# A transformer block on one core: four gate units as seven half-size products (Strassen) in place of eight

## What is computed

```python
proj = xn @ w_in                       # 1024 x 4808
qa, ka, va, qi, ki, wi, qb, kb, vb, ga, gb = split(proj)
oa = dsa_attention(...)                # sparse attention, keys chosen by the scores of qi, ki
ob = stick_breaking_attention(qb, kb, vb)
merged = sigmoid(ga) * (oa @ w_proj_a) + sigmoid(gb) * (ob @ w_proj_b)
h = x + merged @ w_out
h = h + moe_ffn(rms_norm(h))           # 32 experts, 12.58 MB of weights each
```

## Time and profile before

| | |
|---|---|
| median of 3 runs | 1138.24 us (1136.64 to 1138.38) |
| the profiled execution | 1135.92 us, span 1134.1 us |
| TensorE busy | 1090.9 us, 96% of the span |
| VectorE, ScalarE, GpSimd busy | 262.5, 139.7, 8.4 us |
| TensorE clock granted, mean | 0.989 |
| HBM read | 434.89 MB, 384 GB/s over the span |

### The profile page before, as it was taken

One profiled execution on the slowest core, in us unless ns is written; L12 is line 12 of the kernel. 1 busy time (PEld: TensorE's weight loads), 2 busy tenths in 40 slices (PEclk: granted clock), 3 DMA queues, 4 the chain that ended last, 5 costly groups with the idle time before them and its releaser, 6 DMA issues.

```text
span 1134.1 us, 11423 instructions
## 1 busy us (share of the span) xinstructions
PE 1090.9 (96%) x5083; PEld 478.5 (42%) x5083; DVE 262.5 (23%) x619; ACT 139.7 (12%) x237; POOL 8.4 (1%) x16
## 2 busy tenths in 40 slices
PE   8999999999999999999999979999999999999997
PEld 5677778443333333333333324333333333333332
DVE  2665323242111111111111111221111111111111
ACT  1415332010000000000000000000000000000001
POOL 0100000000000000000000000000000000000000
PEclk9999999999999999999999998999999999999999
DMA  8365447799999999999999999999999999999996
GB/s 312 156 275 204 189 145 300 296 357 433 431 431 439 431 428 437 435 426 435 428 435 431 428 418 429 427 433 434 431 433 431 432 436 427 431 425 428 428 424 255
DMA packets 21506, 436.69 MB, mean 385 GB/s; under 512 B 2480, under 2 KB 2864, under 8 KB 6384
## 3 DMA queue, kind: packets, MB, share of 16 engines
q1 hardware_dynamic: 20496, 434.22, 90.4%
q10 hardware_dynamic: 960, 1.72, 0.4%
HBM read 434.89 MB, written 1.05 MB: 384 GB/s over the span
## 4 chain that ended last, share of the span: by engine, by line
PE 70%; DMA 24%; DVE 2%; SPq 2%; ACT 1%; issue 0%; ACTq 0%; DVEq 0%
PE Pp L927 31%; DMA gate_up_room<-in_w_gate_up 19%; PE Bp L941 11%; PE Pp L635 7%; PE Ap L955 3%; DMA odd_down<-in_w_down 3%; PE Pp L623 3%; PE Pp L809 2%; PE Ap L820 2%; PE Bp L913 2%; SPq L436 2%; DMA odd_down<-in_b_down 1%; PE Bp L934 1%; DVE odd_down L1457 1%; PE Pp L662 1%; PE Pp L869 1%
## 5 line engine op out<-in xcount | busy, mean ns | idle before, releaser
L927 PE MATMUL Pp<-gate_up_room,OBT 128*64 128x512 f32 x2048 | 453.3, 601 | 17.4 <-DMA gate_up_room<-in_w_gate_up 17.3
L927 PEld LDWEIGHTS Pp<-gate_up_room,OBT 128*64 128x64 f32 x2048 | 147.5, 139 | 307.1 <-issue 279.0
L1446 DVE TENSOR_SCALAR odd_down<-Pp 128x512 f32<-128x512 f32 x31 | 21.4, 692 | 622.2 <-PE Pp L927 622.2
L941 PE MATMUL Bp<-even_down,odd_down 128*64 128x512 f32 x512 | 113.7, 596 | 1.2
L941 PE MATMUL Bp<-odd_down 128*64 128x512 f32 x480 | 106.3, 595 | 1.8 <-DVE odd_down L1457 0.6
L635 PE MATMUL Pp<-odd_down,gate_up_room 128*128 128x256 f32 x384 | 85.2, 381 | 0.0
L1654 ACT ACTIVATE odd_down<-odd_down 128x512 f32<-128x512 f32 x30 | 18.9, 630 | 473.4 <-DVE odd_down L1446 473.4
L635 PEld LDWEIGHTS Pp<-odd_down,gate_up_room 128*128 128x128 f32 x384 | 72.2, 190 | 10.7 <-issue 1.1
L955 PE MATMUL Ap<-odd_down,cst 64*128 64x512 f32 x256 | 64.7, 624 | 4.9 <-DMA odd_down<-in_b_down 4.2
L941 PEld LDWEIGHTS Bp<-even_down,odd_down 128*64 128x64 f32 x512 | 35.2, 137 | 69.0 <-issue 63.3
L941 PEld LDWEIGHTS Bp<-odd_down 128*64 128x64 f32 x480 | 33.2, 137 | 65.3 <-issue 59.9
(11 more groups left out here) (209 smaller groups left out, 624.4 us busy)
## 6 DMA issues: line engine op xcount, KB each, us to landing
gate_up_room<-in_w_gate_up SPq DMA_DIRECT2D x27, 2048.0 KB, 42.5
even_down<-in_w_down SPq DMA_DIRECT2D x11, 4096.0 KB, 37.0
odd_down<-in_w_down SPq DMA_DIRECT2D x11, 4096.0 KB, 40.2
gate_up_room<-in_w_gate_up SPq DMA_DIRECT2D x10, 4096.0 KB, 22.0
gate_up_room<-in_w_in SPq DMA_DIRECT2D x8, 2048.0 KB, 7.4
even_down<-in_w_down SPq DMA_DIRECT2D x7, 2048.0 KB, 16.7
odd_down<-in_w_down SPq DMA_DIRECT2D x6, 2048.0 KB, 20.3
odd_down<-in_w_down SPq DMA_DIRECT2D x7, 1024.0 KB, 21.0
```

The source lines that it names most:

```text
L927: last = mm((Gps, Ups)[q // 2][64 * (q % 2):64 * (q % 2) + 64, :], xT[:, k % 4, k // 4, :], quarter(e, w, q), start=False, stop=k == KC - ...
L941: last = mm(bank[64 * hf:64 * hf + 64, :], turned[:, c, s, :], w[:, c * 1024 + hf * 512:][:, 0:512], start=s == 0 and c == 0, stop=s == DN ...
```

## The change

The product (2 x 2 blocks: feature block f of 256, contraction half k of 512, token block b of 128) is done for each pair of feature chunks, 128 features of each f, by seven products of 128 features x 512 x 128 tokens in place of eight, after Strassen (Winograd's form). GpSimd forms four differences of tokens once (`XS`, in the room of the bias rows) and four sums of weights per unit (`weight_sum`, in ring slots 0, 1 or 2, 3 by turns). ScalarE copies two partial results aside (`keep_products`), VectorE copies one (`gate_sum_6`), adds (`gate_sum_7`) and writes both chunks (`gate_last`). For each unit `gate_start` and `gate_end` stand where `column_half(u, 0)` and `column_half(u, 1)` stood. The unit's weights have three places now, the loads of units 6 to 9 come earlier, those of w_proj_b and w_out later. The diff, cut; where VectorE's and ScalarE's new calls stand is in its last parts:

```diff
+XS = norm_pair[:, 0:2048].rearrange("p (s k t) -> p s k t", s=4, k=4)
+kept = [cst[:, C_ADM:C_ADM + 384], once[:, 1624:2008]]
...
-    flat = slot(2, 0, 4096) if u == 2 else unit[:, u % 2, :]
+    flat = {2: slot(2, 0, 4096), 6: slot(4, 0, 4096), 7: unit[:, 0, :], 8: unit[:, 1, :],
+            9: slot(4, 0, 4096)}.get(u, unit[:, u % 2, :])
...
-    flat = unit[:, 0, :] if u == 10 else slot(4, 0, 4096)
+    flat = unit[:, u - 10, :]
...
+def weight_quarter(u, f, k):
+    return uview(u)[:, 4 * k:4 * k + 4, 256 * f:256 * f + 256]
+def weight_sum(u, i):
+    return slot(u % 2 * 2, 1024 * (i - 1), 1024).rearrange("p (k n) -> p k n", k=4)
+def token_quarter(k, b):
+    return XT[:, 4 * k:4 * k + 4, b * P:(b + 1) * P]
+def gate_chunk(t, f):
+    u = 6 + t // 2
+    return G[:, 4 * (u % 2) + t % 2 + 2 * f, (u - 6) // 2, :]
...
-    for u in range(11):
+    for u in (0, 1, 2, 3, 4, 6, 5, 7, 8, 9, 10, 11, 12):
         if u >= 3:
-            sp.wait_ge(m_half, 4 if u == 3 else 2 if u == 4 else 2 * (u - 1))
+            sp.wait_ge(m_half, {3: 4, 4: 2, 5: 8, 6: 2, 7: 10, 8: 12, 9: 14, 10: 16, 11: 18, 12: 18}[u])
...
-        if u >= 5 and u < 8:
-            load_unit(u + 6)
...
     for i in (1, 2, 3):
         load(0, i)
     load_half(0, 5, 1)
-    sp.wait_ge(bias_ok, 2)
+    sp.wait_ge(m_half, 20)
+    load_unit(13)
     load_half(1, 5, 0)
-    sp.wait_ge(m_half, 20)
+    load(0, 0)
+    sp.wait_ge(m_mg, KC)
     load(1, 1)
-    sp.wait_ge(m_mg, KC)
-    load(0, 0)
     load_half(0, 5, 0)
     load(1, 0)
...
+    def difference(dst, a, b, op, done):
+        nc.gpsimd.tensor_tensor(dst, a, b, op).then_inc(done, 1)
+    pool.wait_ge(v_sx, KC)
+    pool.wait_ge(bias_ok, 2)
+    difference(XS[:, 0], token_quarter(0, 1), token_quarter(0, 0), ALU.subtract, g_xs)
+    difference(XS[:, 2], token_quarter(1, 1), token_quarter(0, 1), ALU.subtract, g_xs)
+    pool.wait_ge(g_xs, 2)
+    difference(XS[:, 1], token_quarter(1, 1), XS[:, 0], ALU.subtract, g_xs)
+    pool.wait_ge(g_xs, 3)
+    difference(XS[:, 3], token_quarter(1, 0), XS[:, 1], ALU.subtract, g_xs)
+    for u in range(6, 10):
+        pool.wait_ge(unit_in[u], 16)
+        if u > 6:
+            pool.wait_ge(m_half, 6 if u == 7 else 2 * (u - 1))
+        n = 4 * (u - 6)
+        difference(weight_sum(u, 1), weight_quarter(u, 1, 0), weight_quarter(u, 1, 1), ALU.add, g_ws)
+        pool.wait_ge(g_ws, n + 1)
+        difference(weight_sum(u, 2), weight_sum(u, 1), weight_quarter(u, 0, 0), ALU.subtract, g_ws)
+        pool.wait_ge(g_ws, n + 2)
+        difference(weight_sum(u, 4), weight_quarter(u, 0, 1), weight_sum(u, 2), ALU.subtract, g_ws)
+        difference(weight_sum(u, 3), weight_quarter(u, 0, 0), weight_quarter(u, 1, 0), ALU.subtract, g_ws)
...
+    def product(t, part, w, x, start, stop):
+        f = slice(t % 2 * P, t % 2 * P + P)
+        for k in range(4):
+            last = mm(Pp[:, t % 2, part * P:(part + 1) * P], w[:, k, f], x[:, k, :], start=start and k == 0,
+                      stop=stop and k == 3, skip_group_check=True)
+        return last
...
+    def gate_products_15(t, u):
+        if t % 2 == 0:
+            pe.wait_ge(unit_in[u], 16)
+        product(t, 2, weight_quarter(u, 0, 0), token_quarter(0, 0), True, False)
+        if t == 0:
+            pe.wait_ge(g_xs, 4)
+        if t % 2 == 0:
+            pe.wait_ge(g_ws, 4 * (u - 6) + 1)
+        product(t, 1, weight_sum(u, 1), XS[:, 0], False, False).then_inc(m_p15, 1)
+    def gate_products_63(t, u):
+        pe.wait_ge(a_p15, t + 1)
+        if t % 2 == 0:
+            pe.wait_ge(g_ws, 4 * (u - 6) + 3)
+        product(t, 2, weight_sum(u, 2), XS[:, 1], False, False)
+        product(t, 1, weight_sum(u, 4), token_quarter(1, 1), False, True).then_inc(m_p63, 1)
+    def gate_product_7(t, u):
+        pe.wait_ge(v_p6, t + 1)
+        if t % 2 == 0:
+            pe.wait_ge(g_ws, 4 * (u - 6) + 4)
+        product(t, 2, weight_sum(u, 3), XS[:, 2], False, False).then_inc(m_p7, 1)
+    def gate_products_42(t, u):
+        pe.wait_ge(v_p7, t + 1)
+        product(t, 2, weight_quarter(u, 1, 1), XS[:, 3], False, True)
+        product(t, 0, weight_quarter(u, 0, 1), token_quarter(1, 0), False, True).then_inc(m_half, 1)
...
+    def gate_start(u):
+        a, b = 2 * u - 12, 2 * u - 11
+        if u == 6:
+            pe.wait_ge(a_half, 11)
+        else:
+            pe.wait_ge(v_gate, a - 1)
+        gate_products_15(a, u)
+        if u == 6:
+            pe.wait_ge(a_half, 12)
+        else:
+            pe.wait_ge(v_gate, a)
+        gate_products_15(b, u)
+        gate_products_63(a, u)
+    def gate_end(u):
+        a, b = 2 * u - 12, 2 * u - 11
+        gate_products_63(b, u)
+        gate_product_7(a, u)
+        gate_product_7(b, u)
+        gate_products_42(a, u)
+        gate_products_42(b, u)
...
-    column_half(6, 0)
+    gate_start(6)
     pe.wait_ge(a_half, 12)
     b_values(0)
     b_logits(1)
-    column_half(6, 1)
+    gate_end(6)
     b_sums(1)
-    column_half(7, 0)
+    gate_start(7)
     b_values(1)
     b_logits(2)
     turn_probabilities(1, 1)
-    column_half(7, 1)
+    gate_end(7)
     b_sums(2)
     a_values(1, 0, 1)
     head_products(QAT, KAT, 0, 2, P).then_inc(m_lg, 1)
-    column_half(8, 0)
+    gate_start(8)
     b_values(2)
     b_logits(3)
-    column_half(8, 1)
+    gate_end(8)
     b_sums(3)
     turn_probabilities(0, 2)
-    column_half(9, 0)
+    gate_start(9)
     b_values(3)
     a_values(0, 2, 2)
-    column_half(9, 1)
+    gate_end(9)
 
...
-            pe.wait_ge(a_half, nhalf[0] - 1 + c)
+            pe.wait_ge(v_gate, 7 + c)
...
+    def gate_sum_6(t):
+        dve.wait_ge(m_p63, t + 1)
+        V.tensor_copy(kept[t % 2][:, 2 * P:3 * P], Pp[:, t % 2, 2 * P:3 * P]).then_inc(v_p6, 1)
+    def gate_sum_7(t):
+        dve.wait_ge(m_p7, t + 1)
+        V.tensor_tensor(gate_chunk(t, 1)[:, P:2 * P], kept[t % 2][:, 0:P], Pp[:, t % 2, 2 * P:3 * P],
+                        ALU.add).then_inc(v_p7, 1)
+    def gate_last(t):
+        dve.wait_ge(m_half, 13 + t)
+        V.tensor_copy(gate_chunk(t, 1)[:, 0:P], Pp[:, t % 2, 2 * P:3 * P])
+        V.tensor_tensor(gate_chunk(t, 0), kept[t % 2][:, P:3 * P], Pp[:, t % 2, 0:2 * P], ALU.add)                    .then_inc(v_gate, 1)
...
     select_keys(0, P)
+    gate_sum_6(0)
+    gate_sum_6(1)
+    gate_sum_7(0)
+    gate_sum_7(1)
     b_softplus(1)
+    gate_last(0)
+    gate_last(1)
+    b_argument(1)
     normalise(SEQ, 1)
-    b_argument(1)
+    gate_sum_6(2)
     out_of_bank(m_pt, 1, W2, Ap[:, :, :].rearrange("p a n -> p (a n)"), v_pt)
+    gate_sum_6(3)
+    gate_sum_7(2)
+    gate_sum_7(3)
     b_softplus(2)
+    gate_last(2)
+    gate_last(3)
...
     out_of_bank(m_pv, 2, OAT[:, :, 0:P], Ap[:, 2, :].rearrange("p (j q) -> p j q", j=NP2), v_pv)
+    gate_sum_6(7)
+    gate_sum_7(6)
+    gate_sum_7(7)
+    gate_last(6)
+    gate_last(7)
...
-    def gate_half(u, hf):
-        ab, c = (u - 6) // 2, 4 * ((u - 6) % 2) + 2 * hf
-        evacuate((G[:, c:c + 2, ab, :], 0, 512, 1.0))
+    def keep_products(u):
+        for t in (2 * u - 12, 2 * u - 11):
+            act.wait_ge(m_p15, t + 1)
+            A(kept[t % 2][:, 0:2 * P], Pp[:, t % 2, P:3 * P], ACT.Copy).then_inc(a_p15, 1)
...
-    gate_half(6, 0)
+    keep_products(6)
     b_out(0)
     b_log(1)
     a_exp(SEQ, 1)
-    gate_half(6, 1)
     b_exp(1)
...
-    gate_half(9, 1)
-    act.wait_ge(a_half, nh[0])
+    act.wait_ge(v_gate, 8)
     for i in range(4):
         gi = G[:, 2 * i:2 * i + 2, :, :].rearrange("p c r t -> p (c r t)")
         A(gi, gi, ACT.Sigmoid).then_inc(a_sig, 1)
```

More of the change, by code:

```diff
@@ L272, in hybrid_block @@
         m_half, a_half = sem("m_half"), sem("a_half")
+        g_xs, g_ws = sem("g_xs"), sem("g_ws")
+        m_p15, m_p63, m_p7 = sem("m_p15"), sem("m_p63"), sem("m_p7")
+        a_p15, v_p6, v_p7, v_gate = sem("a_p15"), sem("v_p6"), sem("v_p7"), sem("v_gate")
         v_roti, v_rota = sem("v_roti"), sem("v_rota")
@@ L1308, in _ @@
             mask_logits(0, P, Ap[:, 2:4, :].rearrange("p a (j s) -> p (a j) s", j=NP2), 2)
+            gate_sum_6(4)
+            gate_sum_6(5)
+            gate_sum_7(4)
+            gate_sum_7(5)
             b_softplus(3)
+            gate_last(4)
+            gate_last(5)
             normalise(P, 2)
@@ L1312, in _ @@
             out_of_bank(m_pt, 2, W2[:, 0:1024], Ap[:, 0:2, :].rearrange("p a n -> p (a n)"), v_pt)
+            gate_sum_6(6)
             out_of_bank(m_pv, 2, OAT[:, :, 0:P], Ap[:, 2, :].rearrange("p (j q) -> p j q", j=NP2), v_pv)
+            gate_sum_6(7)
[3 more added lines that the diff above has]
+            gate_last(7)
             for c in range(KC):
@@ L1621, in _ @@
             a_exp(SEQ, 1)
-            gate_half(6, 1)
             b_exp(1)
-            gate_half(7, 0)
+            keep_products(7)
             b_out(1)
             b_log(2)
-            gate_half(7, 1)
             b_exp(2)
-            gate_half(8, 0)
+            keep_products(8)
             b_out(2)
@@ L1632, in _ @@
             a_exp(P, 2)
```

(6 more changed lines are left out.)

## The result

The changed kernel takes 1142.24 us (median of 6 runs, 1140.12 to 1144.67); the kernel before, on the same chip, 1137.87 us. The ratio is 1.0042, with a 95% interval of 1.0029 to 1.0055: slower by 4.8 us (3.3 to 6.3; the two medians differ by 4.4). The profiled execution took 1141.51 us, its span is 1139.6 us.

A forecast was written before the change was run, and what follows sets the result against it. TensorE's time up to the end of unit 9 was taken to set the end; -5.8 + 5.5 + 2.1 + 1.1 = +2.9 us on the median 1138.24 gave 1141.0 us, range 1131.6 to 1143.2.

The forecast's parts named there:

- the products: TensorE's gates in units 6 to 9: 448 half-size products at 112 ns, 50.2 us against 56.0, 5.8 us less.
- first stall: Before the transposes at 67.01 us: GpSimd's eight operations delay VectorE's rotation (v_rota), TensorE waits 5.5 us.
- second stall: Before b_sums(0): unit 7's sums go between VectorE's score operations, v_bs comes late, TensorE waits 2.1 us.
- third stall: Before product 7 of unit 6: VectorE's work and first copy finish late, TensorE waits 1.1 us.
- clock behind the first stall: Lower TensorE clock after the wait at 67 us: 0 in the sum, 1.7 us for the upper bound.
- hand-overs by ScalarE: Inside the gate units: ScalarE loses half-unit evacuations and gains copies half as long, 0 us.
- transfers: Unit loads moved earlier, w_proj_b and w_out later; idle DMA room of 18.4 us absorbs them, 0 us.
- One for one to the end: A microsecond TensorE saves or loses before 170 us moves the full weight stream and the end by a microsecond.
- rival A: VectorE keeps its turn, GpSimd works only in its pauses, no stall: 1132.4 us, chance 0.30.
- B: GpSimd gets every second turn beside VectorE, stall 2.3 to 4.6 us: some 1135.9 us, chance 0.17.
- C: Moved transfers hold the output projection or first experts up and the end stays: 1138.2 us, chance 0.03.
- D: Half-size products are paced by their weight loads, up to 218.8 ns each: 1180 us, chance 0.02.

The follow-up runs named there:

- x1_no_gpsimd: The changed kernel without GpSimd's differences and sums, products taking quarters of weights and tokens directly, so gate values differ: 1131.41 us, ratio 0.9961.
- x4_late: The changed kernel with GpSimd's differences waiting for VectorE's index scores (v_sum) and unit 7's sums for the maskings (v_bs): 1131.02 us, ratio 0.9954.
- x8_after_again: The changed kernel once more, unaltered, one execution for a second profile: 1143.73 us.
- x5_late_first: The changed kernel with only the differences and unit 6's sums made to wait (v_sum): 1134.51 us, ratio 0.9980.
- x6_late_second: The changed kernel with only unit 7's sums made to wait for the first softplus (v_bs): 1139.83 us, ratio 1.0031.
- x3_memset: The kernel before with eight added GpSimd memsets from 53 us, about as long as the differences and sums: 1136.24 us, ratio 1.0000.
- x2_burst: The kernel before with eight added GpSimd subtractions beside the rotation, four of 128x512 and four of 128x1024: 1142.9 us, ratio 1.0060.

## Why the prediction came out right, step by step

The forecast was 1141.0 us with 1131.6 to 1143.2; measured is 1142.24, and the likeliest case (GpSimd holds VectorE, TensorE stalls) is what happened. (The forecast's own lower bound is added up wrongly: 1141.0 - 3.2 - 1.5 is 1136.3, not 1136.6; nothing hangs on it.) Against its own before, the forecast said +2.9 (1141.0 against 1138.24), the measurement +4.8 us. The sum is 2.0 us short, and that it is no further off is luck in part: the three stalls came out 2.3 us smaller than forecast, which hides more than half of two losses of clock (1.69 and 1.62 us), of products that gave 0.75 us less and of 0.26 us around b_sums(0).

| step | forecast, us | measured, us |
|---|---|---|
| the products | -5.8 | -5.05 (the gates' -3.89 less the wait of 1.16); -5.31 in x1_no_gpsimd and x4_late; both with a wait 0.24 shorter |
| first stall | +5.5 | +4.4 |
| second stall | +2.1 | +0.8 |
| third stall | +1.1 | +1.16, by another way |
| clock behind the first stall | 0 (bound 1.7) | +1.69 |
| first expert's clock | not foreseen | +1.62 |
| b_sums(0) and the way to it | 0 | +0.26 |
| hand-overs by ScalarE | 0 | the 1.16 above |
| transfers | 0 | 0 |
| sum | +2.9 | +4.89 |

**One for one to the end: right.** In the eight timed kernels of the table the two stretches add up to what the ratio gives (times 1137 us) within 1.3 us, over a spread of 12 us (-5.3 to +6.7). And behind the first expert nine of eleven profiles agree within 0.9 us.

**Products: right, slightly mis-sized.** 64 of them take 7.24 us (166.40 to 173.64), 113 ns each, 448 some 51 us, where 112 ns gave 50.2. The estimate of 72.6 us by the spacing of 81 ns in the Trainium skill ("TensorE: Matmul & The Clock Gate", Back-to-back issue gap), by which the kernel would have been 16.6 us slower, the trace doesn't bear out.

**First stall: right mechanism, turns counted wrong.** I let GpSimd take a turn before each linked group. It takes one before each of eight single instructions, seven with both operands in SBUF and the TENSOR_SCALAR of 18 columns; a ninth between them (56.06, 0.76 us) went through unheld. Eight instructions grew by 12.3 us, where I had 13.5 (14.0 less 0.5), so v_rota came at 71.86 and not 72.5; TensorE asked for it at 67.5. Rivals A and B predicted no stall at 67 us and fell with it.

**Second stall: right place, wrong way, and with it the clock.** I put unit 7's sums between three of the score operations. They began at 89.08 us, just behind them. Before b_sums(0), VectorE's timeline:

```profile
86.07 2.68 DVE L1348 SCALAR_TENSOR_TENSOR even_down<-gate_up_room,sm,even_down 128x128 f32<-128x128 f32 x7
...
93.44 0.96 DVE L1396 SCALAR_TENSOR_TENSOR gate_up_room<-Bp,gate_up_room 128x768 f32<-128x768 f32 x1 [4.69 <-ACT gate_up_room L1734]
94.43 4.63 DVE L1399 TENSOR_TENSOR gate_up_room<-gate_up_room,odd_down 128x256 f32<-128x256 f32 x2
98.99 2.27 DVE L1382 TENSOR_TENSOR gate_up_room<-Ap,even_down 128x2048 f32<-128x2048 f32 x1
```

The two maskings, each with both operands in SBUF, took 4.63 us in place of 0.76. The row above them reads one operand from PSUM and wasn't held; the row below starts after the last sum has ended (98.77).

That v_bs came at 99.06, near the forecast 99.2, is luck, for I had VectorE's own queue set it. But VectorE stood idle for 4.69 us before these rows, released by ScalarE (L1734), which works on TensorE's logits (88.59 us here, 82.02 before). So v_bs follows TensorE, and the first stall and the clock move both sides of the wait. What is left as second stall is the growth of the maskings, 3.87 us, less the cover that was there before (91.58 - 88.62 = 2.96 us): an estimate of 0.9 us. Measured are 0.80, in x8_after_again 0.97, and in x5_late_first, which has no first stall and no lost clock behind it, 0.99. This is the step at which my clock term went wrong: I let it shrink the second stall (2.1 to 0.4, so "0 in the sum"), and it shrank nothing. Its 1.69 us count in full.

**Third stall: another step that failed.** That 1.1 was forecast and 1.16 measured is luck. I had TensorE wait for VectorE's `gate_sum_6(0)` before product 7, and ScalarE's copies at 0. It waited earlier, for ScalarE, whose timeline says why:

```profile
104.68 0.84 ACT L1738 ACTIVATE gate_up_room<-gate_up_room 128x768 f32<-128x768 f32 x1 [4.43 <-DVE gate_up_room L1405]
105.43 0.37 ACT L1754 ACTIVATE cst<-Pp 128x256 f32<-128x256 f32 x1
```

The copy (L1754) for which `gate_products_63` waits stands in ScalarE's queue behind `b_exp(0)` (L1738), which waited 4.43 us for VectorE's `b_argument(0)`, late because the maskings were. ScalarE wasn't busy; it stood behind a late engine. x6_late_second, with the maskings back at 0.76 us, has no such wait. My zero had counted ScalarE's work and not what stands ahead of it.

**Transfers: right.** Moved loads cost nothing in x1 and x4.

**First expert: not in the prediction.** 1.62 us. Its cause is open.

**The rivals.** C and D fell as well: no stream effect, no product at more than 114 ns. What rival A gave for undisturbed turns, 5.8 us less than before, is about what x4_late reaches by timing instead (5.2 less).

## What to carry to other kernels

Work handed to GpSimd because it is idle is free only where VectorE has none of the work that was held here (both operands in SBUF, or a TENSOR_SCALAR from SBUF to SBUF), and where TensorE doesn't want the result of that work soon. Lay both timelines side by side, count one VectorE instruction for each GpSimd instruction, and then delay GpSimd by one wait past the critical stretch: here this turned +4.8 us into -5.2 us. A queue that is free is not a hand-over at no cost: look at what the instruction ahead of it waits for.

## What the runs showed of the hardware

**Turns.** From 53.6 to 70 us GpSimd's eight instructions and VectorE's held ones take turns, eight against eight held and one that went through: GpSimd's take 16.3 us (6.12 + 10.22) against 14.7 in x4_late, where VectorE meets it little (5.19 + 9.54). Uncontended a difference costs 1.30 and a sum 2.39 us.

**Which instructions are held.** By GpSimd's two-operand instructions: VectorE's with both operands in SBUF, and its TENSOR_SCALAR from SBUF to SBUF (1.19 us for 0.18); not those with an operand in PSUM (128x2048 in x4_late at 87.83 us, beside unit 7's sums: 2.28 us, as before), and not the key selection's either (in x4_late the MAX8 and MATCH_REPLACE8 rows beside the weight sums have 0.43 and 0.41 us). By memsets, of what ran beside them in x3_memset: TENSOR_SCALAR and copies from SBUF to SBUF alone. The Trainium skill, "SBUF — State Buffer" (Who interferes with whom), says that two SBUF inputs contend with a GpSimd instruction that reads, not with one that only writes, and that copies and TENSOR_SCALAR can enter modes in which they contend with GpSimd too; x2_burst and x3_memset agree on both counts. I had taken one-operand work for free of it.

**The clock.** In the four profiles with a wait of 4.3 to 4.4 us on TensorE the granted clock fell to 0.50, the lower level: in the changed kernel just behind the wait, in the other three 0.8 to 2.5 us before its end (estimates from stretches of 1 us). It cost 1.7 to 3.0 us: half of the 3.4 to 6.1 us at the lower level in which TensorE worked.
